# Two transformer blocks: inverse norms by split products of a full array, the context's norm inside the second feed-forward block's output groups, scan outputs added straight into X

## The reference

```python
def rmsnorm(x, g):
    x32 = x.astype(jnp.float32)
    y = x32 * lax.rsqrt(jnp.mean(x32 * x32, axis=-1, keepdims=True) + EPS)
    return (y * g.astype(jnp.float32)).astype(x.dtype)

def swiglu(h, w_in, w_out):
    gate, up = jnp.split(h @ w_in, 2, axis=-1)
    return (jax.nn.silu(gate) * up) @ w_out

def mla_qkv(p, prm, pos):
    ...
    q = (rmsnorm_2(q_a, prm['g_qa']) @ prm['w_q_up']).reshape(B, L, MLA_HEADS, MLA_QK)
    ...
    q = rmsnorm_2(q, prm['g_q'])      # 8 heads of 96 features
    k = rmsnorm_2(k, prm['g_k'])
```

## Time and profile before

| | us |
|---|---|
| median of 3 runs | 2797.7 |
| the three runs | 2794.1, 2797.7, 2799.02 |
| the profiled execution, its own time | 2793.76 |
| its span | 2791.9 |
| PE busy in the span | 2509.2 (90%) |
| DVE busy | 1799.2 (64%) |
| ACT busy | 1047.4 (38%) |

### The profile page before, as it was taken

The page is one execution under the profiler, slowest core; times in us unless marked ns, Lnnn a source line. Parts: engine busy times, 40 slices in busy tenths (PEclk is TensorE's granted clock), DMA queues, the critical chain, the costliest instruction groups (busy, mean ns, idle before and its releaser), DMA issues.

```text
span 2791.9 us, 34645 instructions
## 1 busy us (share of the span) xinstructions
PE 2509.2 (90%) x13004; PEld 1887.0 (68%) x13004; DVE 1799.2 (64%) x3296; ACT 1047.4 (38%) x1932; POOL 422.3 (15%) x563
## 2 busy tenths in 40 slices
PE   6899999799997999799988899989789998988997
PEld 1788787555886899433443788878557676757775
DVE  1785686586746877323657565565468887565896
ACT  2322222233232443211233222222247785264884
POOL 1111110100001111000200344334102220000220
PEclk9899999899999999899998899999999999998999
DMA  6466654242234687111011000000038996205996
GB/s 246 164 201 201 198 197 141 95 143 83 83 122 165 222 279 269 46 45 53 31 38 38 1 1 1 1 1 1 16 107 307 347 322 236 87 13 161 327 341 211
DMA packets 115047, 386.72 MB, mean 139 GB/s; under 512 B 20160, under 2 KB 22336, under 8 KB 114624
## 3 DMA queue, kind: packets, MB, share of 16 engines
q1 hardware_dynamic: 76640, 276.33, 29.0%
q0 software_dynamic: 34848, 95.47, 10.5%
q10 hardware_dynamic: 3392, 12.70, 1.2%
HBM read 389.66 MB, written 26.21 MB: 149 GB/s over the span
## 4 chain that ended last, share of the span: by engine, by line
PE 48%; DVE 15%; DMA 8%; ACT 6%; issue 3%; POOL 1%; DVEq 0%; ACTq 0%; SPq 0%; POOLq 0%
PE ps L143 47%; DMA RG<-in_w 6%; DVE moe0wl L152 2%; DVE moe1wl L152 2%; PE ps L146 1%; DMA AR<-in_a 1%; DVE acc L160 1%; DVE rwMM L172 1%; ACT moe1wh L149 1%; ACT moe0wh L149 1%; DVE H L160 1%; DVE rwa L152 1%; ACT gqaas L149 1%; DVE f2wl L152 0%; DVE X L160 0%
## 5 line engine op out<-in xcount | busy, mean ns | idle before, releaser
L143 PE MATMUL ps<-H,RG 128*128 128x256 f32 (+2 forms) x1088 | 361.3, 488 | 15.4 <-ACT H L149 15.2
L160 DVE SCALAR_TENSOR_TENSOR acc<-AR,cs,acc 128x512 f32<-128x512 f32 x420 | 295.8, 747 | 49.0 <-DMA AR<-in_a 46.8
L143 PEld LDWEIGHTS ps<-H,RG 128*128 128x128 f32 (+1 forms) x1088 | 205.5, 192 | 157.1 <-issue 132.8
L152 DVE TENSOR_TENSOR moe0wl<-RG,moe0wh 128x1024 fp32r<-128x1024 f32 x144 | 173.5, 1220 | 37.5 <-ACT moe0wh L149 33.2
L199 POOL DMA_DIRECT2D AR<-in_a x152 | 81.9, 539 | 660.2 <-DVE acc L160 500.8
L149 ACT ACTIVATE moe0wh<-RG 128x1024 fp32r<-128x1024 f32 x144 | 150.7, 1061 | 68.9 <-DMA RG<-in_w 43.8
L152 DVE TENSOR_TENSOR rwXX<-rwXX,ps 128x512 f32<-128x512 f32 x144 | 92.5, 643 | 111.6 <-PE ps L143 111.6
L152 DVE TENSOR_TENSOR moe1wl<-RG,moe1wh 128x1024 fp32r<-128x1024 f32 x120 | 144.7, 1220 | 23.1 <-ACT moe1wh L149 21.5
L149 ACT ACTIVATE f1wh<-RG 128x1024 fp32r<-128x1024 f32 x66 | 70.0, 1061 | 235.6 <-PE ps L143 235.5
L143 PE MATMUL ps<-f1hh,f1wh 128*128 128x512 f32 x352 | 143.4, 408 | 8.7 <-DVE f1hl L152 8.7
L149 ACT ACTIVATE moe1wh<-RG 128x1024 fp32r<-128x1024 f32 x120 | 126.1, 1061 | 47.5 <-DMA RG<-in_w 29.7
(11 more groups left out here) (628 smaller groups left out, 6124.4 us busy)
## 6 DMA issues: line engine op xcount, KB each, us to landing
RG<-in_w SPq DMA_DIRECT2D x525, 512.0 KB
AR<-in_a POOLq DMA_DIRECT2D x152, 512.0 KB, 4.0
moe0back<-moe_outs ACTq DMA_DIRECT2D x4, 1024.0 KB, 8.0
CT<-in_consts ACTq DMA_DIRECT2D x1, 2546.0 KB, 18.5
X<-in_x ACTq DMA_DIRECT2D x1, 2048.0 KB, 11.6
moe_rows<-moe0ht POOLq DMA_DIRECT2D x4, 512.0 KB, 5.8
moe1back<-moe_outs ACTq DMA_DIRECT2D x2, 1024.0 KB, 6.4
X<-in_ctx ACTq DMA_DIRECT2D x1, 1024.0 KB, 6.5
```

The source lines that it names most:

```text
L143: return Silent() if self.e is None else self.e.matmul(out, lhs, rhs, start=start, stop=stop, skip_group_check=True)
L152: return Silent() if self.e is None else self.e.tensor_tensor(out, a, b, op)
L160: return Silent() if self.e is None else self.e.scalar_tensor_tensor(out=out, in0=a, scalar=s, in1=b, op0=op0, op1=op1)
```

## The change

1. **Inverse norms.** The 8 rows are split into a rounded part `ih` (ACT) and a rest `il` (DVE), each held in a full [128, 512] fp32r tile whose other rows ACT zeroes at the stage's start, and a head's column of the identity is `pickh`, [128, 8] fp32r, broadcast to [128, 128]. Each of the 16 broadcasts is two fp32r matmuls of the full array.
2. **The last group of every `Glu`** makes its first three outputs together (`LEAD`): for each hidden tile in turn one product into each of three banks, waiting for that tile's `dl` alone. The split of the following chunks is written at the third.
3. **The context's norm of block two** moves into the second feed-forward (`aside`): squares (ACT) and their sum (DVE) in group 1, the product with ones at the head of group 2 on PE, root, refinement, scale and shift in the output steps of group 2. The latents' norm takes its squares and sums as `Post` writes X, and `Pre` "p3" has 256 columns. The norms of the latents use columns 256 to 511 of H. The last modulation set is finished ahead of `Post`; the wait for the second context's load stands ahead of the feed-forward.
4. **`out2` is an `Onto`**: DVE adds gate * bank to X for each output, ACT squares it, PE sums it three outputs later; Z is gone.

```diff
 class Pre:
+    def gains_dve(self, e):
+        ...
     # Glu.put_pe
+        last = ks[-1] == self.nt - 1
+        if last:
+            if self.aside is not None:
+                self.aside.sums.total_pe(e)
+            ...
+            pe_lead(g, e, outs, [[self.down(k, f) for k in ks] for f in range(self.LEAD)],
+                    lambda n: (self.dh[:, ks[n] % 9, :], self.dl[:, ks[n] % 9, :]), lambda n: [self.S.dve.at(("dl", ks[n]))],
+                    [lambda f=f: p.up(("put", q, f)) for f in range(self.LEAD)])
+            g.ws.settle((self.name, "put", q, self.LEAD - 1), p.now())
+        for f in range(self.LEAD if last else 0, KT):
...
+    def aside_act(self, e, q, f, last):
+        n = self.aside
+        if q == 1:
+            n.sums.square_act(e, f, self.g.X[:, f, n.c0:n.c1], [self.S.pe.at(("up", 0))], False)
+        if last and f == 1:
+            n.sums.root_act(e)
+        if last and 3 <= f < 7:
+            n.shifted(e, 2 * f - 6)
+            n.shifted(e, 2 * f - 5)
+
+    def aside_dve(self, e, q, f, last):
+        n = self.aside
+        if q == 1:
+            n.sums.add_dve(e, f)
+        if last and f == 2:
+            n.sums.refine_dve(e)
+            n.gains_dve(e)
+        if last and 2 <= f < 6:
+            n.scaled(e, 2 * f - 4, self.g.AC)
+            n.scaled(e, 2 * f - 3, self.g.AC)
...
     # Ffn.pe, and the same in dve and pool; sets is 2 in the first block, 20 in the second
-        self.ada.need(e, "pe", self.j)
+        self.ada.need(e, "pe", self.sets)
...
     # Mla.pe
-        self.qa.pe(e, [], 1, self.pre.each)
+        self.qa.pe(e, [], 1, lambda k: self.ctx.each(k) + self.pre.each(k))
...
-                e.wait_ge(*S.dve.at(("y", q)))
-                e.matmul(ps[0:96, :], g.C("ident", 8)[:, h:h + 1].broadcast_to([8, 96]), self.nv[0:8, 2 * q + 1, :], True,
-                         True).then_inc(*p.up(("inv", q, h)))
+                e.wait_ge(*S.dve.at(("il", q)))
+                one = self.pickh[:, h:h + 1].broadcast_to([P, P])
+                e.matmul(ps[:, :], one, self.ih[:, q, :], True, False)
+                e.matmul(ps[:, :], one, self.il[:, q, :], False, True).then_inc(*p.up(("inv", q, h)))
     # Mla.act
+        e.activation(self.pickh[:, :], g.C("ident")[:, 0:8], ACT.Copy).then_inc(*a.up())
+        for x in (self.ih, self.il):
+            e.activation(x[:, :, :], g.C("ident")[:, 0:1].unsqueeze(2).broadcast_to([P, 2, T]), ACT.Copy, scale=0.0).then_inc(*a.up("zero"))
...
+            e.wait_ge(*S.dve.at(("y", q)))
+            e.activation(self.ih[0:8, q, :], self.nv[0:8, 1, :], ACT.Copy).then_inc(*a.up(("ih", q)))
     # Mla.dve
+            e.wait_ge(*S.act.at(("ih", q)))
+            e.tensor_tensor(self.il[0:8, q, :], y, self.ih[0:8, q, :].bitcast(F32), SUB).then_inc(*v.up(("il", q)))
...
     # MixerAb
-            self.out2 = Proj(g, S, "out", ada, T, lambda f: [W("ab_w_out_2", k, f * P, (0,)) for k in range(4)],
-                             lambda k: R[:, k, :], lambda f: Z[:, f, :], KT)
-            self.add2 = Gated(g, S, "add", ada, Z, 0, T, 11, after)
+            self.out2 = Onto(g, S, "out", ada, 0, T, lambda f: [W("ab_w_out_2", k, f * P, (0,)) for k in range(4)],
+                             lambda k: R[:, k, :], 11, after)
     # Plan
+        self.pre_ctx = Pre(g, N, "p3c", ada, 0, 256, gain("n1", 0), 9, 10, Sums(g, N, "s7", 256, False))
-                            "ffn2_w_out", gain("norm_post", 16), 8, (3, 1), None)
+                            "ffn2_w_out", gain("norm_post", 16), 8, (3, 1), s_ab, 20)
+            self.ffn2.glu.aside = self.pre_ctx
-        self.pre_ab = Pre(g, N, "p3", ada, 0, T, gain("n1", 0), 9, 10)
+        self.pre_ab = Pre(g, N, "p3", ada, 256, T, gain("n1", 0), 9, 10, s_ab)
```

More of the change, by code:

```diff
@@ L850, in dve @@
         self.sums.inv_dve(e)
-        for tok in self.ada.ready(self.jshift) + self.ada.ready(self.jscale) + needs:
+        for tok in needs:
             e.wait_ge(*tok)
-        e.tensor_scalar(g.AC[:, :, :], g.mod[:, self.jscale, :, :], 1.0, None, ADD).then_inc(*v.up())
-        e.wait_ge(*v.now())
-        e.tensor_tensor(g.AC[:, :, :], g.AC[:, :, :], bc(self.gain, [P, KT, 2]), MUL).then_inc(*v.up())
-        e.wait_ge(*v.now())
+        self.gains_dve(e)
         for k in range(KT):
@@ L864, in dve @@
         v.note((key, "end"))
+    def gains_dve(self, e):
+        g, v = self.g, self.S.dve
+        for tok in self.ada.ready(self.jshift) + self.ada.ready(self.jscale):
+            e.wait_ge(*tok)
+        e.tensor_scalar(g.AC[:, :, :], g.mod[:, self.jscale, :, :], 1.0, None, ADD).then_inc(*v.up())
+        e.wait_ge(*v.now())
+        e.tensor_tensor(g.AC[:, :, :], g.AC[:, :, :], bc(self.gain, [P, KT, 2]), MUL).then_inc(*v.up())
+        e.wait_ge(*v.now())
     def scaled(self, e, k, gains):
@@ L1082, in __init__ @@
         self.tmp = g.sb(st, name + "tmp", [P, 2, N])
-        self.pre = None
+        self.pre = self.aside = None
     def group(self, q):
@@ L1122, in put_pe @@
         g, p, N, ks = self.g, self.S.pe, self.N, self.group(q)
-        for f in range(KT):
+        last = ks[-1] == self.nt - 1
+        if last:
+            if self.aside is not None:
+                self.aside.sums.total_pe(e)
+            outs = []
+            for f in range(self.LEAD):
+                outs.append(g.banks.take((self.name, "put", q, f))[:, 0:N])
+                for tok in g.banks.free((self.name, "put", q, f)):
+                    e.wait_ge(*tok)
+            pe_lead(g, e, outs, [[self.down(k, f) for k in ks] for f in range(self.LEAD)],
[3 more added lines that the diff above has]
+        for f in range(self.LEAD if last else 0, KT):
             key = (self.name, "put", q, f)
@@ L1215, in put_dve @@
                 self.sums.add_dve(e, f - 2)
+            if self.aside is not None:
+                self.aside_dve(e, q, f, ks[-1] == self.nt - 1)
             if ks[-1] < self.nt - 1:
@@ L1895, in pool @@
         self.glu.pool(e)
-        self.ada.need(e, "pool", self.j)
+        self.ada.need(e, "pool", self.sets)
         self.post.pool(e)
@@ L3811, in dve_program @@
     p.mixer1.dve(e)
+    e.wait_ge(g.s_ctx2, 16)
     p.ffn2.dve(e, [])
```

72 lines of the change are left out of this document (40 added, 32 removed).

## The result

| | before | after |
|---|---|---|
| median | 2797.7 us | 2757.0 us |
| all runs of the first comparison | 2794.1 to 2799.0 (4) | 2746.0 to 2763.0 (4) |
| the profiled execution, its span | 2791.9 | 2758.6 |

The ratio of the two is 0.9852, with a 95% interval of 0.9817 to 0.9887. In a second comparison, with six runs of the changed kernel beside eleven of the one before, it is 0.9856 (0.9831 to 0.9881), with medians of 2764.3 and 2800.3. So the change is worth 36 to 41 us by the medians. The forecast was 2762.2 us, 35.5 less than before, in a range of 2755 to 2772. In the first comparison the changed kernel's runs differ by 17 us, the runs of before by 5; the mean granted clock of the four goes from 0.952 to 0.960, and the fastest run has the highest.

The account below looks back on a forecast made before the run. The prediction saw stretches where engines wait for one another or PE runs at the lower clock; gains 16.2 + 2.6 + 12.1 + 2.2 + 2.4 = 35.5 us off the 2797.7 median gave 2762.2 us, range 2755 to 2772.

Parts of the forecast that it names:

- Inverse norms: MLA: full-array pairs keep the upper clock, DVE's scaling sets the pace, the projection behind ends 16.2 us earlier.
- the Trainium skill's sentence: Inverse norms: PE idling briefly between groups while cycling PSUM banks makes the clock swing; would give the first rival's sum.
- the first rival: Inverse norms: the clock falls all the same, gain 7.7 in place of 16.2, time 2770.7 us; chance 0.09.
- The transition: Second feed-forward to mixer: last X to MLA's first product takes 5.0 us against 17.1, gain 12.1 (10.0 to 12.8).
- The second feed-forward's end: Last group: the `dl` wait and low clock go, a split wait of about 1.4 appears; gain 2.6 (0 to 4).
- the 0.6 for the upper clock: Second feed-forward's end: Post's sum may see the upper clock since PE no longer stands long; up to 0.6 us.
- the second rival: Second feed-forward: aside work starves it, PE stands 3.88 again and group 1 loses 2.5; 2770.1 us; chance 0.11.
- The first feed-forward's end: PE no longer waits 2.22 us after the modulation's matmuls for the last hidden tile's split; gain 2.2.
- The range of 1.1 to 4.4: First feed-forward's end: gain 1.1 if the low clock ends at the same instant, 4.4 if it isn't there.
- Scan output: Scan output into X: four sums stand inside the projection, the eighth ends at 2044.0 instead of 2046.5; gain 2.4.
- the lower end: Scan output: gain of only 1 us if ACT's three chunk splits set the root.
- The other rivals: Scan loses its clock (60 us at 0.50: 2816; chance 0.03); only transition or only MLA works as said (2774.3; 0.05).

Follow-up runs that it names:

- experiments 5: Changed kernel with every inverse-norm pair of full-array matmuls made twice (64 records); one execution, 2765.7 us.
- experiment 6: Changed kernel with every inverse-norm pair made twice, but using 8 rows of the array instead of 128; one execution, 2781.0 us.
- 7: Changed kernel with the inverse norms as 16 f32 matmuls of the full array, without the split; one execution, 2762.0 us.
- experiment 8: Changed kernel with DVE scaling each head twice, so that PE waits for banks in the inverse norms; one execution, 2763.9 us.
- experiments 2: Changed kernel with the norm ahead of block two as before: one norm of 512 columns, nothing of it in the second feed-forward; 2769.2 us, ratio 0.9880.
- 3: Changed kernel with the last group of both feed-forwards made output by output (LEAD = 0); 2765.3 us, ratio 0.9877.
- experiment 1: Changed kernel with the inverse norms as before: 16 f32 matmuls of 8 rows, no zeroed tiles; 2777.7 us, ratio 0.9920.

## Why the prediction was right

**Inverse norms, 16.2 forecast, 16.3 measured.** Each step held: DVE began to scale 1.7 us after the first record (forecast 1.35), at one scaling per 0.66 us (0.65 to 0.80, 0.70 taken); the projection began after 7.8 us (7.65), took 7.05 (7.11), and the rope began after 14.7 (14.75). The two small misses cancel. One reason was not as told: the text has DVE set the pace (the ninth scaling at 7.65), and the ninth scaling did end after 7.68 us, but PE, never waiting, needed 7.8 for its 32 records (7.2 forecast; from the first record to the second alone 0.64 pass). The two came so close that it made no difference. The reason given, that the full array keeps the clock up, is shown by experiments 5 and 6, and 7 shows that the format has no part in it. But it was only half of what the runs show. The text set the Trainium skill's sentence against the rows, and said that by it the pairs would lose the clock since they "give their banks to DVE by turns". In fact the pairs never waited for a bank, so the sentence did not apply, and where they were made to wait (experiment 8) it was right. With a DVE half as fast the clock falls as the first rival says, but the place is then DVE's 32 scalings long (22.8 us), whatever the clock does.

**The transition, 12.1 forecast, 12.3 measured.** 4.9 us from the end of the last X to the first product, 5.0 forecast from the first feed-forward's end. This was a reading of a place that already works the new way, and the safest term of the sum.

**The second feed-forward's end, 2.6 forecast, 2.5 measured** in this execution, 2.3 by the mean of nine. The last addition of squares ends at 1127.41, 22.6 us after the last product of `hh` instead of 25.0: the 2.4 of the text. The wait for a split was forecast at 1.4 and is 1.21; by the count of records it falls into the fifth output (the expectations call it the fourth). Post's sum ran in 1.12 us, so next to none of the 0.6 for the upper clock came. Group 1 cost nothing. The wait at the third output (0.14 here, up to 1.27 elsewhere) is missing in the text, and it is small in this execution by chance. The parts within the term are larger than its sum shows (4.6 gained and 2.1 lost, experiments 2 and 3), and the second rival, aside work that starves the feed-forward, is true to the extent of these 2.1.

**The first feed-forward's end, 2.2 forecast, 2.9 measured**, and 1.3 in two of the other executions. Against the modulation's matmuls the restart moved by 2.36 us (4.14 to 1.78); what differs is how long the lower clock lasts behind it, 3.7 us here, 4.4 before. The range of 1.1 to 4.4 holds all of them. Of the 2.9 only 1.1 reached the second feed-forward's start in this execution, since mixer one's first products ran longer at the lower clock; the text did not count on that.

**Scan output, 2.4 forecast, 2.7 measured.** The eighth sum ended 36.8 us after the first product, 37.0 forecast. ACT's three chunk splits and DVE's two do stand ahead of the root and the refinement, as the lower end feared, but they did so before.

**The other rivals.** The scan did not lose its clock, it reads 1.00; and every part does what it says.

**The sum** was 1.2 low by places. The remaining 4 us between the forecast and the median of the first comparison (2757.0) are within what the clock does from run to run: the second comparison has 36 by its medians (2764.3), on the forecast's other side. So that a whole run comes within 2 or 5 us of 2762.2 is in part chance; the places are what bears the forecast out.

## What to carry to other kernels

A run of matmuls that use few rows of the array (8 here) can cost twice what its columns say, and leave the lower clock to what follows; padding with zeros to the full array cost two copies on an otherwise free ACT and gave 10 of the 16 us. Look for "8*96" and the like in the rows, and at the clock in the window, not at the busy share, which was full in both cases. Whoever lets a slower engine empty the banks should count whether PE gets to wait before its run ends: here eight banks and 0.66 against 0.46 us were just enough. And a norm at a stage border is cheapest when half of it can be made early and the squares of the rest as the tiles come, but what is put into the stage ahead is paid there in part (2.1 us here, of 12.7 gained).

## What was not expected

- The clock fell with PE busy without a break, and how soon differs: after 5.5 us of 8-row f32 matmuls before, 2.7 in experiment 1, 2.6 in the fp32r form of experiment 6. So the same instructions cost 3.4 us more in one execution than in another.
- Stands of 0.54 to 0.59 us between pairs of 0.73 were followed by the lower clock (experiment 8), with the array full in every record.
- Twelve short records in a stand kept the clock up over the 2.44 us that remained of it.
- The executions of either kernel spread over 17 to 18 us in the second comparison (2751 to 2769, 2793 to 2810). Some 5 of them can lie in the scan alone, with the same code.
